# Applying a norm's factors behind the products instead of ahead of them, in a two-layer streaming encoder

## The chip, the cores and the metric

The kernel runs on one core of a Trainium2 chip. TensorE (PE) multiplies, VectorE (DVE), ScalarE (ACT) and GpSimd (POOL) work on tiles, and SyncE (SP) issues most of the loads. The metric is the time of one execution in microseconds; a run's time is a median over executions. Times of instructions are from one execution that the hardware profiler recorded.

## What is computed

Two groups of rows (512 prompt positions and 64 sample positions, 576 in all) go through two layers that share their weights. Cut to what matters here:

```python
def rmsnorm(x, g):
    y = xf * lax.rsqrt(jnp.mean(xf * xf, axis=-1, keepdims=True) + EPS)
    return (y * g)
...
h = x + 0.5 * rmsnorm(swiglu(rmsnorm(x, f1_pre), f1_up, f1_down), f1_post)      # FFN 1
mix, new = token_mix(rmsnorm(h, m_pre), ..., w_in, ...)                         # mixer
h = h + rmsnorm(mix, m_post)
h = h + 0.5 * rmsnorm(swiglu(rmsnorm(h, f2_pre), f2_up, f2_down), f2_post)      # FFN 2
e = pe @ ple_w
h = h + rmsnorm(e * sigmoid(rmsnorm(h, ple_pre) @ ple_gate_w), ple_post)        # PLE
```

The model width is 1024, the FFN width 2816. `swiglu` is silu(a) * b of two halves of one product. The mixer's input projection makes the inputs of four branches and four gates. All is float32 in and out.

## The kernel before

**Layout.** Activations lie with features on the partitions: `h` is 8 tiles (k = 0 to 7) of 128 features x 576 rows. A row's norm factor is therefore one number for each column, spread to all partitions by small matmuls.

**Products.** A weight unit is 1024 x 128 (8 tiles k). For the precision, weights and inputs are each split into a high and a low part (`whi`, `wlo`; `u_hi`, `u_lo`), and `products` (L598) runs high x high, high x low and low x high for each k, in two halves of 288 columns: 6 matmuls for each tile k, 48 for a unit. Units go through four slots: SP loads `wraw`, ACT rounds it to `whi` (`act_round`, L560), POOL subtracts to `wlo` (`split`, L2017; `wlo` lies where `wraw` was), PE multiplies, and its end (`unit_done`) frees the slot for the load of the unit four later. Products land in one of four pairs of PSUM banks.

**Norms.** At the end of FFN 1, mixer, FFN 2 and PLE stands a norm of that stage's result (`pe_norm_y`): ACT squares, DVE adds the squares, PE sums over partitions with a matrix of ones (`token_sums`, L630, 10 matmuls for a tile of 576 rows), ACT takes the root, DVE the reciprocal, PE spreads it (`spread`, L638, 10 matmuls). DVE then makes `uf` = y * gain * factor tile by tile (L846), and DVE or POOL add it to `h` (L838; POOL tiles 1, 3, 4, 6, DVE the rest). Right behind it stands the norm of the next stage's input (`pe_norm_h`): ACT squares each new tile of `h`, PE sums it (8 x 10 matmuls), root, reciprocal and spread again, DVE makes `uf` = h * gain * factor (L829, the factor read from PSUM), ACT copies it to `u_hi` (L747), and DVE (tiles 0, 3, 7) or POOL (1, 2, 4, 5, 6) subtracts to `u_lo` (L823). Only then do the first products of the stage have their tile; `wait_k` makes the first unit wait tile by tile. `keep_clock` issues dummy matmuls (L615) in pauses of PE.

**Stages.** The FFN's up loop runs 11 times over four units (a, b, a, b of two pairs): ACT takes silu of a's PSUM, DVE multiplies by b's PSUM, and splits into `s_hi`, `s_lo`; down units of 1024, 1024 and 768 rows follow. The mixer runs five projections (`FILL0`: two forget gates F, two queries Q, the first value V), each drained by ACT (`act_proj_some`, L928 and on), then the recurrent branch with further projections as fill. The order of every engine is written out by hand; an engine's instructions run in their order, with semaphore waits between engines.

**The start** of the first layer: SP loads the rows in five pieces and then the weights; PE transposes them (L456), DVE copies them to `h`, squares are added on DVE, and one `pe_norm_y` follows. 15 small loads of gains, taps and other rows are issued by ACT first of all.

Of the kernel before, what the change touches and what calls it, by code (L numbers as in the profile page):

```python
# [70 lines left out]
LO_POOL, LO_DVE = (1, 2, 4, 5, 6), (0, 3, 7)  # L71
ADD_POOL, ADD_DVE = (1, 3, 4, 6), (0, 2, 5, 7)
# [7 lines left out]

R_CONVB, R_LNG, R_LNB = range(3)
N_TAPS = DEPTH * CW * 2
N_ROWS = 9 * DEPTH
N_ROW_LOADS = 16
# [3 lines left out]
def trunk(nc, a, o):  # L88
    n_consts = [0]
    n_late = [0]  # L90
    with ExitStack() as ctx:
# [68 lines left out]


# [21 lines left out]
        hgs0 = rh("hgs0", [2, HD])  # L183
# [17 lines left out]
        rbc = Region(limit - 8192 - 32)  # L201
        sbk_c = rbc("sbk_c", [4, 256])
        sbv_c = rbc("sbv_c", [4, 256])
        assert rs.at <= limit - 8224
# [3 lines left out]
        spx = rb("spx", [2, 512])  # L208
        arg = rb("arg", [2, 512])

# [24 lines left out]
        rr = Region(ru.at)  # L235
        prow = rr("prow", [3, 128])
        prow_end = rr.at
        xtok = Region(prow_end)("xtok", [TB, D])
        otok = Region(ru.at + 3 * KD * T * 4)("otok", [TB, D])
        alibi_neg = Region(limit - 4096)("alibi_neg", [WINDOW + CHUNK])  # L240
# [10 lines left out]
        def halves(ap):  # L251
# [8 lines left out]
        turned = sem("turned")  # L260
        placed = sem("placed")
# [19 lines left out]
        h_ready_pool = sem("h_ready_pool")  # L281
        u_full = sem("u_full")
# [84 lines left out]
            h_ready: 16, h_ready_pool: 16, u_full: 32, u_high: 32, u_ready: 12, u_ready_pool: 20,  # L367
# [14 lines left out]
        ROW_BANKS = (0, 4, 5)  # L382

        def setup_sync(sp_):
            sp_.dma_start(xtok[0:DEC, NT, :], a["x_sample"][0]).then_inc(tok_loaded, 16)
            for c in range(4):
                f = slice(D // 4 * c, D // 4 * (c + 1))
                sp_.dma_start(xtok[:, 0:NT, f], a["x_prompt"][0].rearrange("(t p) d -> p t d", p=128)[:, :, f]).then_inc(x_loaded[c], 16)

# [56 lines left out]
        def setup_tensor(pe):  # L446
            pe.wait_ge(consts_done, 2)
            pe.wait_ge(tok_loaded, 16)
            for k in range(KD):
                if k % 2 == 0:  # L450
                    pe.wait_ge(x_loaded[k // 2], 16)
                if k >= 4:
                    pe.wait_ge(placed, k - 3)
                for t in range(TB):
                    n = min(128, T - 128 * t)
                    ins = pe.transpose(flat(k % 4)[:, 128 * t:128 * t + n], xtok[0:n, t, 128 * k:128 * k + 128], ident[0:n, 0:n])  # L456
                ins.then_inc(turned, 1)
# [6 lines left out]
        def setup_vector(dve, add_square):  # L464
            for k in range(KD):
                dve.wait_ge(turned, k + 1)
                dve.tensor_copy(h[:, k, :], flat(k % 4)).then_inc(placed, 1)
                if k:
                    add_square(k - 1)
# [1742 lines left out]
```

## Time and profile before

| | us |
|---|---|
| median of 3 runs | 3248.1 (3246.3 to 3248.9) |
| the profiled execution | 3254.2 |
| its span, first to last instruction | 3252.5 |

The page lists, for each engine, its busy time and share of the span. The chain of waits is the work that ended last, followed back from the last instruction; in order of time it reads as start, length, engine, operation and how many instructions were merged. The timeline lists instructions in order of time, merged where alike, with the idle time before them and what ended it. The table of stretches gives for each engine the busy time and number of instructions and then PEclk, the granted TensorE clock as a share of 2.4 GHz (0.50 is 1.2 GHz). TensorE's clock is recorded from 26.6 us on; before that the table shows 1.00 for want of a record. Matmuls overlap, so the time of a run of matmuls is read from start to start.

### The profile page before, as it was taken

The page shows a single profiled execution, that of the slowest core. Times are in us where ns is not written, and L with a number is a line of the kernel's source. Part 1 is how long each engine was busy: PE and PEld are TensorE (multiplying, and loading weights), DVE is VectorE, ACT ScalarE, POOL GpSimd, SP SyncE. Part 2 cuts the span into 40 slices and gives each one's busy share as a digit, 9 for nine tenths or more (in the row PEclk, how much of TensorE's full clock was granted, in tenths as well). Part 3 has the DMA queues.
Part 4 walks back from the last instruction along what each step waited for, and adds up shares of the span by engine and source line. Part 5 has one row for each costly group of instructions (what it writes and reads, how often), then busy time and mean ns, then how long its engine had stood idle before and what let it go on. Part 6 is the DMA issues. An engine that isn't in the chain of part 4 may idle for free.

```text
span 3252.5 us, 55941 instructions
## 1 busy us (share of the span) xinstructions
PE 3149.6 (97%) x24207; PEld 3034.4 (93%) x24207; DVE 964.3 (30%) x1417; ACT 1089.4 (33%) x1544; POOL 1179.3 (36%) x564
## 2 busy tenths in 40 slices
PE   8999999999999999999999999999998999999998
PEld 8999999996799999999999999999867999999997
DVE  3111024744344311101331110248434433111023
ACT  3223222335433323322433222323454333323233
POOL 5434333331133433433443333423212434333333
PEclk9999989999999999999999999999999999999999
DMA  3222212321122222232212222223111222222221
GB/s 102 80 82 82 83 55 63 87 69 48 40 72 79 59 84 83 78 90 80 65 53 83 84 81 80 62 62 92 56 48 46 78 79 59 84 81 87 83 69 62
DMA packets 455968, 236.46 MB, mean 73 GB/s; under 512 B 18630, under 2 KB 454150, under 8 KB 455814
## 3 DMA queue, kind: packets, MB, share of 16 engines
q1 hardware_dynamic: 445792, 227.05, 23.9%
q10 hardware_dynamic: 10022, 7.15, 0.7%
q8 instruction: 122, 2.00, 0.3%
q14 instruction: 32, 0.26, 0.0%
HBM read 228.53 MB, written 5.63 MB: 72 GB/s over the span
## 4 chain that ended last, share of the span: by engine, by line
PE 89%; DVE 5%; ACT 3%; POOL 1%; issue 1%; ACTq 1%; POOLq 0%; DVEq 0%
PE ps L598 79%; PE ps L630 3%; PE ps L1549 1%; PE ps L638 1%; DVE uf L829 1%; PE ps L1529 1%; PE ps L1567 1%; DVE u_lo L823 1%; PE ps L1868 1%; ACT u_hi L747 1%; POOL u_lo L823 1%; DVE kgate L1140 0%; PE ps L1553 0%; ACT ybr L1728 0%; PE ps L1391 0%
## 5 line engine op out<-in xcount | busy, mean ns | idle before, releaser
L2017 POOL TENSOR_TENSOR wlo<-wraw,whi 128x1024 fp32r<-128x1024 f32 (+1 forms) x432 | 1042.0, 2417 | 1918.2 <-ACT whi L560 1917.9
L598 PE MATMUL ps<-u_hi,whi 128*128 128x288 f32 x4800 | 1051.3, 300 | 43.7 <-POOL u_lo L823 11.8
L598 PE MATMUL ps<-u_hi,wlo 128*128 128x288 f32 x4800 | 1032.7, 296 | 0.0
L598 PE MATMUL ps<-u_lo,whi 128*128 128x288 f32 x4800 | 1032.6, 296 | 0.0
L598 PEld LDWEIGHTS ps<-u_hi,whi 128*128 128x128 f32 x4800 | 768.7, 189 | 80.9 <-issue 53.1
L598 PEld LDWEIGHTS ps<-u_lo,whi 128*128 128x128 f32 x4800 | 773.5, 189 | 0.0
L598 PEld LDWEIGHTS ps<-u_hi,wlo 128*128 128x128 f32 x4800 | 773.5, 189 | 0.0
L560 ACT ACTIVATE whi<-wraw 128x1024 fp32r<-128x1024 f32 (+1 forms) x432 | 449.5, 1040 | 562.9 <-PE ps L598 331.9
L872 DVE TENSOR_TENSOR sq<-sq,ps 128x576 f32<-128x576 f32 x88 | 66.4, 754 | 900.2 <-PE ps L598 900.2
L598 PE MATMUL ps<-s_hi,whi 128*128 128x288 f32 x1408 | 303.0, 296 | 0.0
L598 PE MATMUL ps<-s_lo,whi 128*128 128x288 f32 x1408 | 302.6, 296 | 0.0
L598 PE MATMUL ps<-s_hi,wlo 128*128 128x288 f32 x1408 | 302.6, 296 | 0.0
L598 PEld LDWEIGHTS ps<-s_hi,whi 128*128 128x128 f32 x1408 | 226.4, 189 | 0.3
L598 PEld LDWEIGHTS ps<-s_hi,wlo 128*128 128x128 f32 x1408 | 226.5, 189 | 0.0
L598 PEld LDWEIGHTS ps<-s_lo,whi 128*128 128x128 f32 x1408 | 226.3, 189 | 0.0
L560 ACT ACT_TABLE_LOAD x44 | 56.5, 1283 | 420.7 <-PE ps L598 420.7
L813 DVE TENSOR_TENSOR sqsum<-sqsum,sq 128x576 f32<-128x576 f32 x54 | 40.8, 756 | 473.7 <-ACT sq L726 473.7
L1321 DVE SCALAR_TENSOR_TENSOR yc<-zc,taps_all,yc 128x606 f32<-128x606 f32 x120 | 151.1, 1260 | 4.2
L726 ACT ACTIVATE sq<-ps 128x576 f32<-128x576 f32 x48 | 31.3, 652 | 283.6 <-PE ps L598 283.6
L630 PE MATMUL ps<-ones,sq 128*128 128x64 f32 x690 | 90.9, 294 | 6.2 <-ACT sq L726 5.9
L630 PEld LDWEIGHTS ps<-ones,sq 128*128 128x128 f32 x690 | 88.4, 209 | 8.2 <-ACT sq L726 6.8
L598 PE MATMUL ps<-m_split,whi 128*128 128x288 f32 x512 | 89.3, 296 | 0.3 <-DVE m_split L1765 0.3
(271 smaller groups left out, 2586.3 us busy)
## 6 DMA issues: line engine op xcount, KB each, us to landing
wraw<-in_ffn_up SPq DMA_DIRECT2D x176, 512.0 KB, 3.8
wraw<-in_w_in SPq DMA_DIRECT2D x104, 512.0 KB, 3.8
wraw<-in_ffn_down SPq DMA_DIRECT2D x64, 512.0 KB, 4.0
wraw<-in_ffn_down SPq DMA_DIRECT2D x32, 384.0 KB, 3.4
wraw<-in_w_out SPq DMA_DIRECT2D x16, 512.0 KB, 4.0
wraw<-in_ple_gate_w SPq DMA_DIRECT2D x16, 512.0 KB, 4.0
wraw<-in_w_branch SPq DMA_DIRECT2D x16, 256.0 KB, 2.7
xtok<-in_x_prompt SPq DMA_DIRECT2D x4, 512.0 KB, 6.2
```

Source lines behind the costliest of these rows:

```text
L560: act.activation(whi[:, i % SLOTS, 0:width(i)], wraw[:, i % SLOTS, 0:width(i)], ACT.Copy).then_inc(w_rounded, 1)
L598: ins = pe.matmul(ps[:, 2 * p + f, 0:HT], wt[:, part, w], x[:, k, HT * f:HT * f + HT], start=start and n == 0 and c == 0, stop=stop and n ...
L630: ins = pe.matmul(sum_at(p)[:, tb], x[:, t0:t0 + 128], ones[:, 0:SAME], start=start and tb == 0, stop=stop and tb == TB - 1, skip_group_ch ...
L638: ins = pe.matmul(flat(p)[:, t0:t0 + 128 - n0], col(tb), ident[:, n0:128], start=True, stop=True)
L747: act.activation(u_hi[:, k, :], uf[:, k, :], ACT.Copy).then_inc(u_high, 1)
L813: dve.tensor_tensor(sqsum[:], sqsum[:], sq[:, k % 2, :], ALU.add).then_inc(sq_added, 1)
L823: engine.tensor_tensor(u_lo[:, k, :], uf[:, k, :], u_hi[:, k, :], ALU.subtract).then_inc(signal, 1)
L829: dve.scalar_tensor_tensor(out=uf[:, k, :], in0=h[:, k, :], scalar=gains_all[:, n, L, k:k + 1], in1=flat(norm_pair(n)), op0=ALU.mult, op1= ...
L872: dve.tensor_tensor(halves(x), halves(x), pair(2 * q + 1), ALU.mult).then_inc(up_mul, 1)
L1321: ins = dve.scalar_tensor_tensor(out=yc[:, c, :], in0=zc[:, c, w:w + YW], scalar=wc, in1=yc[:, c, :], op0=ALU.mult, op1=ALU.add)
L1529: pe.matmul(ps[:, bk, 0:SEQ - 128 * kb], proj[hh, BK_ + c, 128 * kb:128 * kb + 128], proj[hh, BQ_ + c, 128 * kb:SEQ], start=True, stop=Tru ...
L2017: pool.tensor_tensor(wlo[:, i % SLOTS, 0:width(i)], wraw[:, i % SLOTS, 0:width(i)], whi[:, i % SLOTS, 0:width(i)], ALU.subtract).then_inc( ...
```

## The change

It leaves the arithmetic of a norm as it is but moves its factor, which is one number for each row and commutes with the product, behind the product, for FFN 1, FFN 2 and the mixer's first three projections.

- **Tiles.** `act_tiles` copies h * gain to `u_hi` as soon as a tile of `h` is there, then squares it; DVE's `tile_low` makes `u_lo` = h * gain - `u_hi`. PE's `pe_tiles` goes tile by tile: the sum of squares, then the tile's products of the first *two* units (into pairs 2 and 3); the spread of the factors stands ahead of the last tile. ACT copies the factors to SBUF as `rsb`.
- **FFN.** `gated` on DVE: a * rsb from PSUM, silu on ACT in place, * rsb, * b from PSUM, then the split. Units 0 to 3 stand outside the loops, which run 10 times. PE waits for `up_raw` ahead of the down units.
- **Mixer.** F, F+1 and the first Q run on raw tiles; DVE's `raw` multiplies them by `rsb` into `proj`. While Q runs, DVE makes the full `um` = h * gain * rsb and ACT overwrites `u_hi` behind PE (`u_spent`); `u_lo` is subtracted on DVE (0, 2, 4, 6, 7) and POOL (1, 3, 5). The second Q and all later units use it. ACT takes the sigmoids of F in `act_raw`, behind four cache loads. The recurrent state's load goes to `sqsum`'s place, and the load of `sbk_c` waits for `hg_norm` as well.
- **Residual.** POOL adds tiles 1 to 6, DVE 0 and 7, at all norms. PLE's own input norm stays as it was.
- **Weights around it.** The second unit's `act_round` and `split` stand ahead of the residual in place of behind it.
- **Start.** SP loads the first two units' weights between the rows' pieces; the first gain is loaded and transposed by itself, so `act_tiles` can begin; PE mixes transposes, sums (8 in place of 2) and the first unit's tiles. The other 15 row loads are issued by ACT behind the first rounds, and their transposes, copies and the bounds stand at the end of the first up loop.

```diff
-ADD_POOL, ADD_DVE = (1, 3, 4, 6), (0, 2, 5, 7)
+ADD_POOL, ADD_DVE = (1, 2, 3, 4, 5, 6), (0, 7)
+LO_POOL = {N_MPRE: (1, 3, 5), N_PPRE: (1, 2, 4, 5, 6)}
...
         def setup_sync(sp_):
...
+                if c < 2:
+                    src = a["ffn1_up"][bass.ds(0, 1), :, FF * c:FF * c + 128].rearrange("l (k p) n -> p (l k) n", p=128)
+                    sp_.wait_ge(unit_done, c + 1)
+                    sp_.dma_start(wraw[:, c, :].rearrange("p (k n) -> p k n", k=KD), src).then_inc(w_loaded[c], 16)
...
+                if n != N_F2POST:
+                    keep_clock(pe, 2, 2)
+                factors(pe, n)
...
+                keep_clock(pe, 8, 2)
+                pe.wait_ge(y_normed, 8 * (n // 2) + 1 + before(y_normed))
+                keep_clock(pe, 6, 2)
+                pe.wait_ge(t_high, tile_no(n + 1, 0, L) if n < N_PPOST else tile_no(N_F1PRE, 0, L + 1))
+                keep_clock(pe, 4, 2)
...
+            def pe_tiles(pe, n, i):
+
+                split_ready(pe, i + 1)
                 for k in range(KD):
+                    if k < KD - 1:
+                        h_sums(pe, n, k)
+                    if k == KD - 2:
+                        h_sums(pe, n, k + 1)
+                    if k == KD - 1:
+                        factors(pe, n)
+                    for j in range(2):
+                        tile_products(pe, n, i + j, 2 + j, k)
+
+            def pe_start(pe):
+
+                setup_tensor(pe, 0)
+                setup_tensor(pe, 1)
+                gain_tensor(pe)
+                setup_tensor(pe, 2)
+                h_sums(pe, N_F1PRE, 0)
+                setup_tensor(pe, 3)
+                h_sums(pe, N_F1PRE, 1)
+                split_ready(pe, 0)
+                for k in range(KD):
+                    tile_products(pe, N_F1PRE, 0, 2, k)
+                    if k < 4:
+                        setup_tensor(pe, 4 + k)
+                    if k < 6:
+                        h_sums(pe, N_F1PRE, 2 + k)
+                split_ready(pe, 1)
+                for k in range(KD):
+                    if k == 2:
+                        factors(pe, N_F1PRE)
+                    tile_products(pe, N_F1PRE, 1, 3, k)
...
+            def act_tiles(act, n, rounds):
 
                 for k in range(KD):
+                    wait_h(act, n, k)
+                    act.activation(u_hi[:, k, :], h[:, k, :], ACT.Copy, scale=gains_all[:, n, L, k:k + 1]).then_inc(t_high, 1)
+                    act_square(act, n, k, h[:, k, :])
+                    if k in rounds:
+                        act_round(act, rounds[k])
                 act_root(act, n)
+                act.wait_ge(factors_out, n + 1 + before(factors_out))
+                act.activation(rsb[:], flat(norm_pair(n)), ACT.Copy).then_inc(r_kept, 1)
...
+            def tile_low(dve, n, k, l):
+
+                dve.wait_ge(t_high, tile_no(n, k, l))
+                dve.scalar_tensor_tensor(out=u_lo[:, k, :], in0=h[:, k, :], scalar=gains_all[:, n, l, k:k + 1], in1=u_hi[:, k, :],
+                                         op0=ALU.mult, op1=ALU.subtract).then_inc(t_low, 1)
...
+            def dve_tiles(dve, n, src, n_in, l):
+
+                dve_rstd(dve, n)
+                for k in range(KD):
+                    norm_y_tile(dve, n, src, k)
+                    if k in ADD_DVE:
+                        add_to_h(dve, n, k, h_ready)
+                    if k >= 2:
+                        tile_low(dve, n_in, k - 2, l)
+                tile_low(dve, n_in, KD - 2, l)
+                tile_low(dve, n_in, KD - 1, l)
...
+                    dve.tensor_tensor(halves(x), pair(up_pair(2 * q)), halves(rsb[:]), ALU.mult).then_inc(up_raw, 1)
+                    dve.wait_ge(silu_done, it * 2 + (at + 1) + before(silu_done))
+                    dve.tensor_tensor(x, x, rsb[:], ALU.mult).then_inc(silu_scaled, 1)
+                    dve.wait_ge(silu_scaled, it * 2 + (at + 1) + before(silu_scaled))
+                    dve.wait_ge(unit_done, it * 4 + done(u0 + 2 * q + 1))
+                    dve.tensor_tensor(halves(x), halves(x), pair(up_pair(2 * q + 1)), ALU.mult).then_inc(up_mul, 1)
...
+            RAW_AT = (2, 3, 0)
+
+            def pe_mixer_in(pe):
+                pe_tiles(pe, N_MPRE, U0_PROJ)
+                i = U0_PROJ + 2
+                split_ready(pe, i)
+                for k in range(KD):
+                    ins = products(pe, i % SLOTS, u_hi, u_lo, (k,), k, RAW_AT[2], k == 0, k == KD - 1)
+                    ins.then_inc(u_spent if k < KD - 1 else unit_done, 1)
+                i = U0_PROJ + 3
+                split_ready(pe, i)
+                pe.wait_ge(r_kept, N_MPRE // 2 + 1 + before(r_kept))
+                products(pe, i % SLOTS, u_hi, u_lo, range(KD), 0, 1, True, True, wait_k=u_tile_ready(pe, N_MPRE)).then_inc(unit_done, 1)
+                pe.wait_ge(proj_raw, 3 + before(proj_raw))
+                for t in range(4, FILL0):
+                    pe_proj(pe, t)
+
+            def act_mixer_in(act):
+                act_tiles(act, N_MPRE, {2: U0_PROJ + 2})
+                act_round(act, U0_PROJ + 3)
+                for k in range(KD):
+                    u_high_tile(act, N_MPRE, k)
+                act_round(act, U0_PROJ + 4)
+
+            def act_raw(act):
+                for t in (F_, F_ + 1):
+                    act.wait_ge(proj_raw, t + 1 + before(proj_raw))
+                    act.activation(kgate[:, t, :], proj[:, t, :], ACT.Sigmoid, scale=-1.0)
+                    act.activation(proj[:, t, :], proj[:, t, :], ACT.Sigmoid).then_inc(proj_out, 1)
+                act.wait_ge(proj_raw, 3 + before(proj_raw))
+                act.activation(proj[:, Q_, 0:16], proj[:, Q_, 0:16], ACT.Copy).then_inc(proj_out, 1)
+                next_proj[0] = 3
+
+            def dve_mixer_in(dve):
+                dve_factors(dve, N_MPRE)
+
+                def full(k):
+                    dve.scalar_tensor_tensor(out=um[:, k, :], in0=h[:, k, :], scalar=gains_all[:, N_MPRE, L, k:k + 1], in1=rsb[:],
+                                             op0=ALU.mult, op1=ALU.mult).then_inc(u_full, 1)
+
+                def raw(t):
+                    dve.wait_ge(unit_done, done(U0_PROJ + t))
+                    dve.tensor_tensor(halves(proj[:, t, :]), pair(RAW_AT[t]), halves(rsb[:]), ALU.mult).then_inc(proj_raw, 1)
+
+                full(0)
+                full(1)
+                low(dve, N_MPRE, 0, u_ready)
+                full(2)
+                full(3)
+                low(dve, N_MPRE, 2, u_ready)
+                full(4)
+                full(5)
+                low(dve, N_MPRE, 4, u_ready)
+                full(6)
+                full(7)
+                raw(0)
+                raw(1)
+                low(dve, N_MPRE, 6, u_ready)
+                low(dve, N_MPRE, 7, u_ready)
+                raw(2)
...
                 act.wait_ge(outs, 32 + before(outs))
+                act.wait_ge(hg_norm, 2 + before(hg_norm))
...
                 straight(U_UP, U0_PROJ)
-                split(U0_PROJ)
+                straight(U0_PROJ, U0_PROJ + 2)
                 pool_residual(pool, N_F1POST)
-                split(U0_PROJ + 1)
+                straight(U0_PROJ + 2, U0_PROJ + 4)
                 pool_apply(pool, N_MPRE)
-                straight(U0_PROJ + 2, U0_FFN2 + 1)
+                straight(U0_PROJ + 4, U0_FFN2 + 2)
                 pool_residual(pool, N_MPOST)
```

## Rows read from the trace of the kernel before

**Rows 1.** The page, engine shares: busy us, share of the span, instructions.

```profile
PE 3149.6 (97%) x24207; PEld 3034.4 (93%) x24207; DVE 964.3 (30%) x1417; ACT 1089.4 (33%) x1544; POOL 1179.3 (36%) x564
```

**Rows 2.** The chain of waits, entry of FFN 2, first layer: start, us, engine, what.

```profile
1092.12 1.54 DVE uf L846 x2
1095.10 9.46 PE ps L630 x80
...
1116.85 400.25 PE ps L598 x3000
```

**Rows 3.** The chain of waits, the mixer's two entries.

```profile
458.90 1.54 DVE uf L846 x2
461.88 16.14 PE ps L630 x80
...
499.94 19.45 PE ps L598 x144
...
2074.74 1.54 DVE uf L846 x2
...
2108.13 19.46 PE ps L598 x144
```

**Rows 4.** The chain of waits, the first long run of products.

```profile
36.94 417.84 PE ps L598 x3132
```

**Rows 5.** Timeline, PE at the entry of FFN 2: start, us, line, operation, tiles, count.

```profile
1090.75 1.33 PE L638 MATMUL ps<-ident,rcol 128*128 128x128 f32 x10
1091.92 2.00 PE L615 MATMUL ps<-ident,ones 128*128 128x128 f32 x16
```

**Rows 6.** The chain of waits, products and sums in turn in the PLE stage.

```profile
1551.59 1.64 PE ps L1868 x12
1553.23 4.41 PE ps L630 x40
```

**Rows 7.** Timeline, DVE, ACT and POOL at the entry of FFN 2.

```profile
1108.15 0.76 DVE L823 TENSOR_TENSOR u_lo<-uf,u_hi 128x576 fp32r<-128x576 f32 x1
...
1109.66 0.69 ACT L747 ACTIVATE u_hi<-uf 128x576 fp32r<-128x576 f32 x1 [0.82 <-DVE uf L829]
...
1115.37 1.42 POOL L823 TENSOR_TENSOR u_lo<-uf,u_hi 128x576 fp32r<-128x576 f32 x1
...
1115.40 2.01 DVE L823 TENSOR_TENSOR u_lo<-uf,u_hi 128x576 fp32r<-128x576 f32 x1 [0.75 <-ACT u_hi L747]
```

**Rows 8.** Timeline, ACT and POOL at the second layer's mixer entry.

```profile
2100.06 0.40 ACTq L1793 DMA_DIRECT2D hgs<-in_state_hgrn  x1
...
2101.45 0.69 ACTq L1796 DMA_DIRECT2D swv_c<-in_cache_swa_v  x1
2102.17 1.28 ACT L928 ACT_TABLE_LOAD   x1 [4.19 <-issue]
...
2105.69 2.38 POOL L2017 TENSOR_TENSOR wlo<-wraw,whi 128x1024 fp32r<-128x1024 f32 x1 [6.27 <-ACT whi L560]
```

**Rows 9.** Timeline, PE at the start.

```profile
5.68 10.76 PE L456 MATMUL ps<-ident,xtok 128*128 128x128 f32 x40 [5.68 <-DMA xtok<-in_x_prompt]
...
21.19 2.34 PE L630 MATMUL ps<-ones,sq 128*128 128x64 f32 x10
...
26.43 2.55 PE L615 MATMUL ps<-ident,ones 128*128 128x128 f32 x20
```

**Rows 10.** PE at the lower clock: timeline of products; stretch: busy (x), PEclk, DMA share, GB/s.

```profile
883.71 0.68 PE L598 MATMUL ps<-o_lo,whi 128*128 128x288 f32 x2
884.19 0.68 PE L598 MATMUL ps<-o_hi,wlo 128*128 128x288 f32 x2
...
470.00:474.00 4.00, 4.00 (x21) 0.50 0.00 0
```

**Rows 11.** Timeline, DVE and POOL at the last residual.

```profile
3233.16 1.54 DVE L846 SCALAR_TENSOR_TENSOR uf<-e,gains_all,ps 128x576 f32<-128x576 f32 x2 [1.42 <-PE ps L638]
...
3236.90 5.11 POOL L838 TENSOR_TENSOR h<-h,uf 128x576 f32<-128x576 f32 x3 [0.26 <-DVE uf L846]
```

## What I predict, and how

> **What bounds the kernel now.** I read the page's engine shares first: the tensor engine (PE) is busy for 97% of the span [rows 1]. So only two things can move the time: stretches in which PE does no products, and stretches in which its products run slowly. The chain of waits shows where the first are. In the loops it is products all the way (3000 products in 400.25 us, 0.1334 each, so 6.4 for a unit of 48 [rows 2]), and it leaves PE, or falls back to small matmuls, at every norm. The entry of FFN 2 in the first layer [rows 2] stands for three. Call t0 the start of the first residual operation, 1092.12. Then come the residual, 80 matmuls of square sums (9.46, 0.118 each), the second norm, and the input split tile by tile; tile 6 of the first unit starts at 1116.85. From there 60 products are left in the first two units: 8.0 us, so they end 32.7 after t0. The same pair of lines, 24.7 apart, stands at two more entries (layer 2, FFN 1 and FFN 2). The two mixer entries [rows 3] end their first five units 60.5 and 52.9 after their t0 (499.94 + 19.45 - 458.90, and 2108.13 + 19.46 - 2074.74). The 7.6 between them is the clock: 80 sums took 16.14 in the first. At the kernel's start tile 6 begins at 36.94 [rows 4], so two units end at 44.9.
>
> **FFN entries (three).** Up to t0 nothing changes. After it PE gets a chain of its own. The spread of the factors starts at 1090.75 and 16 dummy matmuls follow from 1091.92 in 2.00 us [rows 5]; now there are 36 (18 calls), at 0.125 each 4.5 us, to t0+4.3. Then eight times a sum (1.18) and a tile's 12 products. A stretch of the PLE stage has just this alternation, 12 products in 1.64 and sums right behind them [rows 6], so I take 1.62. With one spread (1.2): 4.3 + 8 x 2.8 + 1.2 = 27.9. What feeds it is faster. POOL's adds take 1.42, a DVE subtract 0.76, an ACT copy 0.69 [rows 7]; POOL and DVE block one another (the subtract issued 0.03 after a POOL one took 2.01, its own 0.76 behind the other's end), so a tile costs add plus subtract, 2.2 at most, under PE's 2.8. The first tile is ready at about t0+4.4, hidden by the dummies. **Gain 32.7 - 27.9 = 4.8 each, 14.4 in all**; 6 each if a dummy costs 0.11, 4 if each handover costs 0.1.
>
> **Mixer entries (two).** T, the end of the first two units, is again t0+27.9. Unit 2 still runs on raw tiles, to T+6.4. Unit 3 needs the fully normalized input, and here the work has grown: 8 normalizing operations on DVE that now read two SBUF tensors (h and rsb; before, the factor came from PSUM), 5 DVE subtracts, and on POOL a weight split (2.4 [rows 8]) and 3 subtracts. Taken as excluding one another [rows 7], 13 x 0.7 + 2.4 + 3 x 1.4 = 15.7 in one row, from T-0.9, and two PSUM products of 0.75 stand in DVE's queue ahead of the last two subtracts: the last tile is ready at T+16.3, and unit 3 ends at T+17.1, not T+12.8. Unit 4 waits for the third proj_out, and that is behind ACT's queue: last high tile T+14.3, a weight round 1.05, the four cache DMA issues 2.1, the sigmoid table 1.3 [rows 8], four sigmoids and a copy 2.4: T+21.3. PE is idle for four of those microseconds; the first mixer entry lost the clock behind a pause shorter than the 3.0 between its t0 and its first sum [rows 3], so I take a fall here too. Back-to-back products then start 0.24 apart [rows 10], and I add 2.2 to unit 4's 6.4. End: 27.9 + 21.3 + 8.6 = 57.8. **First layer -2.7, second +4.9.** Bounds: without exclusion DVE ends by T+10.4 and ACT's chain gives T+14 with no fall of the clock, 48.3 in all; above, 3 more for a longer fall.
>
> **The start.** Eight square sums come to PE in place of two, and they are mixed with transposes and products. As it was [rows 9]: first transposes at 5.68 behind the input's DMA, 10.76 for eight tiles (1.34 each); a sum of 10 matmuls takes 2.34, some 2.15 without the last one's tail; only at 26.43 do dummies run at 0.128 each. New order: four transposes and two sums, held once by ACT's first square at about 10.3 (the gain row is turned behind two tiles, then copied, then a high tile and the square of 0.7 each), end at 16.0. Then unit 0: 8 x 1.45 (six products at 0.24) + 4 x 1.34 + 6 x 2.15 = 29.9 if the clock stays low, to 45.9. Sums alone left it low: 470 to 474 is busy for 4.00 of 4.00 us at 0.50 [rows 10], and so did transposes and sums from 5.68 to 23.5; the dense spread and dummies behind them lifted it. This loop is transposes and sums for most of its time, work beside which the level stayed low, so I stay with that level until the products run unbroken, from 43 on; at a rise at 47.5, unit 1 has 1.1 tiles behind it, then 6.9 x 0.8 + 1.1: 54.1. **Cost 9.2** against 44.9. With a rise at 20 the same counts at 0.8, 1.18 and 1.34 end at 43.5, a gain of 1.4. The weights ahead of x tiles cost nothing in this: the second x chunk comes one 512 KB load later, and PE is behind with its own work from then on.
>
> The Trainium skill, TensorE: Matmul & The Clock Gate, Part 1, says that sustained matmul activity releases the clock. By that rule the start would run at 2.4 GHz soon after its first transposes, and the sum would be about 11 lower; the busy 4 us at 0.50 [rows 10] speak against it, since there the engine was never idle.
>
> **The end.** POOL gets six of eight residual adds in place of four. After the last norm nothing covers them: t0 is 3233.16, POOL's last add ended at 3242.01 [rows 11]. Six at 1.4 from t0+2.2, with one DVE add between them: t0+11.3, **2.4 later** (1.8 to 3.2), and 22 transposes and the output still follow. At the two PLE entries the same delay hides behind PE's e products and sums; uncovered it would be 2.4 each.
>
> **What I cost at nothing.** (1) FFN gate: DVE has two operations more per pair of units, five at 0.76 plus blocks of 2.4 or less; a pair is 12.8 of PE. ACT's silu waits for the first of them, 0.8 behind the unit, while ACT rounds a weight (1.05) anyway. (2) PE's new wait for up_raw ahead of the down units: the last raw product belongs to the last but one unit, 6.4 earlier. (3) The 15 row loads move on ACT from before the first square to behind the first rounds, at 0.52 an issue [rows 8] 7.8 us; queued behind them are the first silu and the round of unit 4. The first gate then ends some 9 to 10 after unit 1; unit 4 asks for it at 12.8. If that margin goes, it costs its excess once. (4) Bounds and row transposes move to the end of the first up loop: 0.9 of PE, which it also paid before; ACT's Exp and table loads there sit ahead of a round that PE needs two units later. (5) The second unit's split moves ahead of the residual on POOL, its round ahead of the last copy on ACT: both have the last down or output units as cover. (6) ACT's wait for hg_norm ahead of the sbk_c load: the projection copies ahead of it in that queue end later than the factors do.
>
> **Sum.** -14.4 - 2.7 + 4.9 + 9.2 + 2.4 = -0.6 against the profiled execution's 3254.2 (span 3252.5 and 1.7 around it): 3253.6. That execution is 6.1 above the median of the runs, so I carry the difference over: 3247.5, say 3247. If the runs don't have the first mixer's slow sums, its gain turns to +4.9 and this is 3255.
>
> **Rivals.** (a) The clock rises early in the start, since products are a new kind of work there: 10.6 less, 3237. For it: unbroken products raise the clock. Against it: nothing in the stretch is unbroken. (b) The mixer entry is not held by DVE and POOL's exclusion: 9.5 less each, 3228; half of it, 3237. Against: the 2.01 [rows 7]. (c) Slower: a tile loop is entered with the clock low, and its sums keep it there, as they did at the first mixer entry. Place: the gap between the last dummies and the first sum, where the first mixer entry lost it [rows 3]. Price, at the lower level throughout: 8 x (2.15 + 2.9) + 2.2 + 4.3 = 46.9 in place of 27.9, 19 for one such entry: 3266. It decides if the gap grows past what the dummies fill; 18 of them speak against it, one fall in five entries before speaks for it. (d) The loops don't overlap as written, because a tile's inputs are late: 2.2 against 2.8 excludes it on these rows.
>
> **How the numbers follow.** Forecast 0.43, (a) 0.23, (b) 0.12, (c) 0.22. About 0.2%, 6.5 us, is what a measurement of this kernel tells from no change. (a) and (b) are faster by more: 0.35. (c) is slower: 0.22. The range, 3230 to 3262, takes in (a), the half of (b), the upper costs at start, mixer and end together (+8), and leaves out part of (b) and of (c). The forecast's own range is 3240 to 3256.
>
> **What would show it.** FFN entries: two units end at t0+27 to 29, and PE has no gap in the loop. Mixer: unit 4 starts 18 to 22 behind the first two units, with DVE operations of 1.4 to 2 beside POOL's. Start: sums of unit 0 at 0.21 per matmul, granted clock at 1.2 GHz until 46 to 50; two units done at 52 to 56. End: POOL's last add about 11 after its t0. The forecast is wrong if the start's products run at 0.134 before 30, or if any of the five later loops shows 0.24.

## The result: 20 us faster, where no change was forecast

The changed kernel takes 3228.6 us (median of 5 runs, 3225.1 to 3234.2) against 3248.9 beside it: ratio 0.992, 95% interval 0.990 to 0.994. Two later comparisons, both on one chip, gave 0.991 (0.990 to 0.993) and 0.990 (0.988 to 0.993), which are 29 and 32 us: the kernel before had medians of 3257.7 and 3260.2 there. The profiled execution has 3228.6, its span 3226.8; that of before had 3254.2 and 3252.5.

The page, shares of the engines. DVE has 283 us more to do (964.3 before [rows 1]), ACT 95 us less, and PE, the bound, 12 us less:

```profile
PE 3137.4 (97%) x24248; PEld 3030.4 (94%) x24248; DVE 1246.9 (39%) x1584; ACT 993.9 (31%) x1482; POOL 1213.0 (38%) x556
```

The timeline of DVE gives the new t0 of the entries (start, us, line, operation); they answer to 458.90, 1092.12, 2074.74 and 3233.16 [rows 2, 3, 11]:

```profile
456.07 0.81 DVE L972 SCALAR_TENSOR_TENSOR uf<-y,gains_all,ps 128x576 f32<-128x576 f32 x1 [1.42 <-PE ps L683]
...
1084.86 0.81 DVE L972 SCALAR_TENSOR_TENSOR uf<-y,gains_all,ps 128x576 f32<-128x576 f32 x1 [1.42 <-PE ps L683]
...
2053.71 0.81 DVE L972 SCALAR_TENSOR_TENSOR uf<-y,gains_all,ps 128x576 f32<-128x576 f32 x1 [1.42 <-PE ps L683]
...
3205.46 0.81 DVE L972 SCALAR_TENSOR_TENSOR uf<-e,gains_all,ps 128x576 f32<-128x576 f32 x1 [1.42 <-PE ps L683]
```

Cut at these points, the span divides as follows:

| stretch | before | after | change | forecast |
|---|---|---|---|---|
| start and FFN 1, to the first mixer's t0 | 458.90 | 456.07 | -2.8 | +9.2 |
| mixer entry, layer 1, t0 to the end of unit 4 | 60.49 | 53.57 | -6.9 | -2.7 |
| rest of that mixer | 572.73 | 575.22 | +2.5 | 0 |
| FFN 2 and PLE, layer 1, to PLE's norm | 528.76 | 522.60 | -6.2 | -4.8 |
| that norm, to layer 2's t0 | 7.17 | 5.43 | -1.7 | 0 |
| FFN 1, layer 2 | 446.69 | 440.82 | -5.9 | -4.8 |
| mixer entry, layer 2 | 52.85 | 53.46 | +0.6 | +4.9 |
| rest of that mixer | 572.47 | 571.32 | -1.2 | 0 |
| FFN 2 and PLE, layer 2 | 533.10 | 526.97 | -6.1 | -4.8 |
| last t0 to the end | 19.34 | 21.34 | +2.0 | +2.4 |
| sum | | | -25.7 | -0.6 |

The chain of waits shows the entries (start, us, engine, count). At FFN 2, 36 dummies take 4.07 (0.113 each), then a tile takes 2.71 (1095.34 to 1098.05), with no pause of PE in between; from the last tile on, 12 products finish the two units, at 1110.02 + 12 x 0.1333 = 1111.62, t0+26.8 (before: t0+32.7 [rows 2]). At the mixer, DVE's `um` and `u_lo` are the chain up to the fifth unit:

```profile
36.93 273.65 PE ps L643 x2052
...
500.69 8.95 PE ps L643 x54
...
1084.82 4.07 PE ps L660 x36
1095.34 1.65 PE ps L643 x12
1098.05 1.65 PE ps L643 x12
...
1110.02 393.65 PE ps L643 x2952
...
2090.83 2.62 DVE um L1123 x2
2094.78 3.51 DVE u_lo L951 x2
2098.33 8.84 PE ps L643 x54
...
3207.08 4.58 POOL h L994 x3
3213.02 3.24 POOL h L994 x2
3216.30 4.93 PE ps L2327 x22
```

The timeline of PE at the start. A sum of ten matmuls takes 2.39 until 16.5 and 1.33 from 22 on; in between it went from 1.2 to 2.4 GHz. The record of the granted clock begins with the rise, at 19.34, 3.1 us behind the start of the first products:

```profile
14.12 2.39 PE L675 MATMUL ps<-ones,sq 128*128 128x64 f32 x10
16.28 0.83 PE L643 MATMUL ps<-u_hi,whi 128*128 128x288 f32 x2
...
19.14 1.41 PE L675 MATMUL ps<-ones,sq 128*128 128x64 f32 x10
...
20.72 0.42 PE L643 MATMUL ps<-u_lo,whi 128*128 128x288 f32 x2
...
21.98 1.33 PE L675 MATMUL ps<-ones,sq 128*128 128x64 f32 x10
```

### The profile page after: what moved, and what is told of

It reads as the page before. It is cut to its first block, busy times and chain, and to the rows that moved or that the text cites. A ratio compares the mean times of both kernels' runs of the same rounds, so it can differ in the third digit from the quotient of the medians.

```text
span 3226.8 us, 55975 instructions
## 1 busy us (share of the span) xinstructions
PE 3137.4 (97%) x24248; PEld 3030.4 (94%) x24248; DVE 1246.9 (39%) x1584; ACT 993.9 (31%) x1482; POOL 1213.0 (38%) x556
## 4 chain that ended last, share of the span: by engine, by line
PE 91%; DVE 4%; ACT 2%; POOL 1%; issue 1%; ACTq 0%; DMA 0%; SPq 0%; POOLq 0%; DVEq 0%
PE ps L643 81%; PE ps L675 3%; PE ps L1781 1%; PE ps L683 1%; PE ps L1761 1%; PE ps L1799 1%; PE ps L660 1%; PE ps L2098 1%; DVE u_lo L951 1%; DVE kgate L1372 0%; DVE um L1123 0%; PE ps L1785 0%; ACT ybr L1960 0%; PE ps L1623 0%; PE ps L1770 0%
## 5 line engine op out<-in xcount | busy, mean ns | idle before, releaser
L2250 POOL TENSOR_TENSOR wlo<-wraw,whi 128x1024 fp32r<-128x1024 f32 (+1 forms) x432 | 1082.6, 2515 | 1892.8 <-ACT whi L600 1892.4
L1034 DVE TENSOR_TENSOR sq<-sq,rsb 128x576 f32<-128x576 f32 x88 | 211.0, 2397 | 96.0 <-ACT sq L895 96.0
L1032 DVE TENSOR_TENSOR sq<-ps,rsb 128x576 f32<-128x576 f32 x88 | 66.8, 759 | 346.4 <-PE ps L643 341.9
L994 POOL TENSOR_TENSOR h<-h,uf 128x576 f32<-128x576 f32 x48 | 82.3, 1747 | 79.3 <-DVE uf L972 79.3
```

Source lines behind the costliest of these rows:

```text
L994: engine.tensor_tensor(h[:, k, :], h[:, k, :], uf[:, k, :], ALU.add).then_inc(signal, 1)
L1032: dve.tensor_tensor(halves(x), pair(up_pair(2 * q)), halves(rsb[:]), ALU.mult).then_inc(up_raw, 1)
L1034: dve.tensor_tensor(x, x, rsb[:], ALU.mult).then_inc(silu_scaled, 1)
L2250: pool.tensor_tensor(wlo[:, i % SLOTS, 0:width(i)], wraw[:, i % SLOTS, 0:width(i)], whi[:, i % SLOTS, 0:width(i)], ALU.subtract).then_inc( ...
```

## The experiments

All edits are to the changed kernel, unless the text says otherwise. Its own repeats gave 3228.6 and 3227.8.

> The changed kernel, a second profile and more times beside the three mixer runs. The first profile ended the five units of a mixer entry 53.6 and 53.5 us behind t0 (t0: start of the first residual operation), with the clock at 1.2 GHz for 6.83 us in both, and the start's clock rose at 19.34; in another kernel with the same start it rose at 24.07. Expected: the mixer entries within 1 us of 53.5 again; the start's two units at 41 to 45.

Measured: five units end at t0+53.6 (500.97 + 9.05 - 456.38) and t0+53.3 (2095.73 + 8.71 - 2051.10), and the start's clock rises at 19.87. In the 12 profiles with this start the rise lay at 18.5 to 19.9 in eight and at 24.1 to 24.8 in four; the later one, some 8 us behind the first products, costs 2 to 3 us.

**What the clock did in the kernel before.** Two runs of the kernel before: once unedited, once with

```diff
-                    keep_clock(pe, 8, 2)
+                    keep_clock(pe, 14, 2)
```

> The kernel before, a second profile. The first one had its square sums at the lower clock behind the first layer's mixer entry (80 sums in 16.14 us in place of 9.46) and a fall to 1.2 GHz at the start of layer 2 (1620.66 to 1627.49). Theory 1: these falls hang on what the tensor engine did before and come back at the same places; then the changed kernel's gain at the first mixer entry (6.9 us from t0 to the end of the fifth unit) is a gain in every execution. Theory 2: they fall where they like; then the 80 sums take 9.46 here, the entry ends its five units 52.9 behind t0 in place of 60.5, and that part of the gain belongs to one execution alone.

> The kernel before with 14 dummy calls in place of 8 behind the spread of a residual's factors, so that the 1.18 us in which the tensor engine waits for the first square sum are filled; nothing else of the change. If that pause loses the clock at the first mixer entry (80 sums in 16.14 and 16.40 us, 9.45 at the other entries), the sums take 9.45 there too and the kernel is 6 to 7 us faster than before (ratio 0.998), so that about a quarter of the change's gain is the clock alone. If the sums themselves lose it, whatever stands ahead of them: 16 us again, and no change or 0.2 us more for each entry.

The unedited kernel lost the clock at the same places again (80 sums in 16.40 at the first mixer entry, and a fall at 1620.49 ahead of layer 2). With the dummies, the chain of waits of the edited kernel has:

```profile
458.64 3.18 PE ps L615 x28
461.82 9.29 PE ps L630 x80
...
492.11 19.44 PE ps L598 x144
...
1647.79 407.43 PE ps L598 x3132
```

Five units end 52.9 behind t0 (458.68), not 60.5, and the kernel is 7.4 us faster by the medians: ratio 0.9977 (0.9959 to 0.9995). So the 6.9 at the first mixer entry are the clock's, and filling a pause of 1.18 us would have had them without the change. (The profiled execution gained more, 12.6 in its span; the last row alone is 10.4 of it, see the end.)

**What raised it at the start.** First, all transposes and sums ahead of the products:

```diff
-                setup_tensor(pe, 2)
-                h_sums(pe, N_F1PRE, 0)
-                setup_tensor(pe, 3)
-                h_sums(pe, N_F1PRE, 1)
+                for k in range(2, KD):
+                    setup_tensor(pe, k)
+                    h_sums(pe, N_F1PRE, k - 2)
+                h_sums(pe, N_F1PRE, KD - 2)
+                h_sums(pe, N_F1PRE, KD - 1)
                 split_ready(pe, 0)
                 for k in range(KD):
                     tile_products(pe, N_F1PRE, 0, 2, k)
-                    if k < 4:
-                        setup_tensor(pe, 4 + k)
-                    if k < 6:
-                        h_sums(pe, N_F1PRE, 2 + k)
```

> The changed kernel, but at the start the tensor engine does all transposes and square sums first and the first unit's products behind them. In the changed kernel the clock rose at 19.34 us, about 3 us behind the first products (16.28), and two units ended at 41.55. Theory A, products mixed in lift the clock: without them transposes (8 x 1.34) and sums (8 x 2.15) stay slow to about 34, the clock rises some 3 us into the products, and two units end at 48 to 51, so the kernel takes 7 to 9 us more than the changed one (about 3236 to 3238). Rival B, transposes and sums without a pause lift it as well, products or not: the rise comes near 19 again, and two units end at 41 to 43, no change in the time. Rival C, it takes what it took in the kernel before, where the clock rose at 26.64: two units end at about 45, 3 to 4 us more.

The chain of waits of that kernel:

```profile
10.57 2.32 PE ps L675 x10
...
27.94 6.59 PE ps L675 x30
34.53 9.07 PE ps L643 x60
44.66 273.65 PE ps L643 x2052
```

Sums at 0.22 to 0.23 a matmul up to 34.5, the clock up at 36.69, and the long run 7.7 later than in the changed kernel (44.66 against 36.93): theory A. 24 us of transposes and sums without a pause stayed at 1.2 GHz; the same work with a unit's products in it did not, in any of the 12 profiles. The median is 3237.5, ratio 0.993.

Then dummies (`ones` by `ident`) from 1.87 us on, ahead of the input: 16 calls (each is two matmuls in the trace); 8 calls, with 4 more ahead of the first product; 10, with 4 more behind the gain's transpose and 6 ahead of the first product. The last two also round the first units one tile earlier:

```diff
+                pe.wait_ge(consts_done, 3)
+                for _ in range(16):
+                    pe.matmul(ps[:, 2, 0:128], ones[:], ident[:], start=True, stop=True)
...
-                    act_tiles(act, n, {1: 0, 3: 1})
+                    act_tiles(act, n, {0: 0, 2: 1})
```

> The changed kernel with 16 dummy matmuls on the tensor engine ahead of the first transposes, from about 2.0 us, while it waits for the input (5.71). If any unbroken work of the tensor engine lifts the clock, it is up at 5 to 6 us: transposes of 0.80 and sums of 1.18 from there, and two units end at 36 to 38 in place of 41.55, the kernel 4 to 5 us faster than the changed one (3224). If only products lift it, or the wait for the second piece of the input (0.66 at 9.31) drops it again, the rise stays near 19 and nothing changes (3228 to 3229).

> The changed kernel's start with 8 dummy calls (16 matmuls) in place of the 16 calls of the run before, so that they end before the input is there (5.7 us), 4 calls more ahead of the first product, and the first two units' rounds one tile earlier on ACT. In the run with 16 calls the clock rose at 6.67 but fell at 16.91, behind a pause of 1.47 us in which the tensor engine waited for the first unit's low part (POOL), and stayed at 1.2 GHz to 23.73. Theory: it is the pause that lost it. Then here the clock is up from 6 or 7 us to the end of the start, and the 24 merged products that begin at 32.62 to 32.93 in the changed kernel begin at 28 to 30: 3 to 4 us less, 3224 to 3226. Rival: dummies lift the clock only for a while and the start's own mix, with its waits for the input's pieces, can't hold it: a fall between 10 and 20 again, and no gain or up to 1.5 us lost.

> The start of the run with 8 dummy calls, whose clock rose at 5.90 and fell at 9.31 behind two waits for the input of 0.95 and 1.01 us. Here 10 calls stand ahead of the input, 4 behind the gain's transpose and 6 ahead of the first product, so that the tensor engine has work in all three places. If the pauses are what drops the clock, it stays up from 6 us on and the 24 merged products begin at 28 to 30 in place of 32.5 to 33.2: 3 to 4 us less than the changed kernel. If it falls again between 9 and 20 with the pauses filled, pauses are not the cause, and the start gains nothing (33 to 35).

The dummies lifted the clock at 6.67, 5.90 and 4.87. It fell at 16.91, 9.31 and 11.70, each time in or up to 2 us behind a pause of about 1 us or more, and came back at 23.73, 19.55 and 18.52. The timelines of PE, 16 calls first:

```profile
15.93 0.53 PE L643 MATMUL ps<-u_hi,whi 128*128 128x288 f32 x2 [1.47 <-POOL wlo L2250]
...
18.02 2.39 PE L675 MATMUL ps<-ones,sq 128*128 128x64 f32 x10
```

8 calls:

```profile
6.60 1.62 PE L485 MATMUL ps<-ident,xtok 128*128 128x128 f32 x10 [0.95 <-DMA xtok<-in_x_prompt]
...
9.39 1.41 PE L485 MATMUL ps<-ident,xtok 128*128 128x128 f32 x5 [1.01 <-DMA xtok<-in_x_prompt]
```

10 calls:

```profile
9.69 0.86 PE L485 MATMUL ps<-ident,xtok 128*128 128x128 f32 x5 [1.05 <-DMA xtok<-in_x_prompt]
...
12.89 2.39 PE L675 MATMUL ps<-ones,sq 128*128 128x64 f32 x10
```

The faster PE only waits longer, for the input or for POOL's split, and the clock falls there. The run that the changed kernel begins at 36.93 began at 38.30, 38.05 and 37.34: nothing gained. The medians are 3231.5, 3227.0 and 3225.5, with ratios of 0.991, 0.991 and 0.990 to the kernel before, as for the changed kernel. That pauses are the cause isn't proved, since each of the three kernels kept one.

**What held it at the entries.** The 18 dummy calls behind the spread taken out, with the two waits that stand between them:

```diff
-                keep_clock(pe, 8, 2)
...
-                keep_clock(pe, 6, 2)
...
-                keep_clock(pe, 4, 2)
```

> The changed kernel without the 36 dummy matmuls behind each spread of a residual's factors, so the tensor engine stands idle for some 4 us ahead of each of the five tile loops. My third rival of the prediction says that a tile loop entered at the lower clock stays there: 19 us for each of five, about 95 more than the changed kernel (3323). Against it stands the start of the changed kernel, where the same mix of sums and products went from 1.2 to 2.4 GHz by itself some 3 us behind the first products: then a loop begins slow and costs 2 to 4 each, 10 to 20 in all (3239 to 3249). If 4 us of pause don't drop the clock, nothing changes (3228).

The median is 3247.7, ratio 0.9967 (0.995 to 0.998): 19 us of the gain gone by the medians; in the profile 17.0, of which the start's rise at 24.07 has 2.4 and the last norm 2.7. The chain of waits at the first mixer entry: one sum and one tile at the lower level, then 1.65 a tile.

```profile
461.55 2.36 PE ps L675 x10
463.92 2.99 PE ps L643 x12
...
471.16 1.65 PE ps L643 x12
```

From the norm's sums to the loop's last sums the five entries took 2.2, 2.3, 4.0, 0.9 and 2.4 more. The loop lifts its own clock, as the start did. The prediction's rival (c) was right that a loop can be entered with the clock low, and wrong that its sums keep it there and in its price, 19 for one entry.

**One unit in the loop instead of two.**

```diff
-                    for j in range(2):
-                        tile_products(pe, n, i + j, 2 + j, k)
+                    tile_products(pe, n, i, 2, k)
+                for k in range(KD):
+                    tile_products(pe, n, i + 1, 3, k)
```

> The changed kernel with one unit in the tile loops (sum and 6 products for each tile, 1.85 us) and the second unit behind the loop. Theory: the loop of the changed kernel is bound by the tensor engine (2.71 a tile, no pause), and its feed by DVE and POOL runs at about 1.9 a tile; with one unit the loop follows the feed, its last tile is there at about t0+18.2 and the spread has less work in front of it, so two units end at t0+27 to 28.5 in place of 26.6: 0.5 to 2 for each of five entries, 3 to 9 us in all (3231 to 3237). Rival 1: the feed is faster than the loop needs: no change. Rival 2: the loop's small waits drop the clock: 3 or more for each entry, over 15 in all.

The median is 3253.5, ratio 0.9996 (0.998 to 1.001): the gain is gone. At FFN 2 a tile takes 1.91 (1096.51 to 1098.42 in the timeline). That is what a sum and six products need and also the pace of the feed, whose DVE subtracts start 1.9 apart. At tile 5 the feed falls behind and PE waits, while DVE takes 4.36 for its last three subtracts:

```profile
1096.51 1.22 PE L675 MATMUL ps<-ones,sq 128*128 128x64 f32 x10
...
1098.42 1.22 PE L675 MATMUL ps<-ones,sq 128*128 128x64 f32 x10
...
1107.57 0.53 PE L643 MATMUL ps<-u_hi,whi 128*128 128x288 f32 x2 [2.20 <-DVE u_lo L967]
```

DVE's timeline there:

```profile
1104.61 4.36 DVE L967 SCALAR_TENSOR_TENSOR u_lo<-h,gains_all,u_hi 128x576 fp32r<-128x576 f32 x3
```

Two units end at t0+29.2 at the FFN entries (1112.71 + 54 x 0.1333 - 1090.74), 2.4 later than with two; at the mixer entries the clock falls behind that wait (475.22 and 2079.48) and they lose 5.7 and 5.9 (at the FFN entries the same wait did not drop it). The 2.4 goes the way of the theory, beyond its 0.5 to 2; the mixer's part is rival 2. The second unit is what hides the feed.

**The mixer entry, cut into its chains.** The subtracts first; the loads behind the sigmoids; both; then the subtracts first and no wait for ACT:

```diff
+                low(dve, N_MPRE, 6, u_ready)
+                low(dve, N_MPRE, 7, u_ready)
                 raw(0)
                 raw(1)
-                low(dve, N_MPRE, 6, u_ready)
-                low(dve, N_MPRE, 7, u_ready)
...
+                act_raw(act)
                 act.dma_start(hgs0, a["state_hgrn"][bass.ds(L, 1), 0].rearrange("l (c a) k v -> (a k) (l c) v", a=2)).then_inc(cache_in, 16)
...
-                act_raw(act)
...
-                if t >= 2:
+                if t > 4:
                     pe.wait_ge(proj_out, t - 1 + before(proj_out))
```

> The changed kernel with DVE's two subtracts for the last two tiles of the mixer's input (L951, 3.5 us for both beside POOL's weight split) ahead of its two products of raw results (1.4), not behind them. Theory A, the fifth unit is held by two chains that end within 0.5 us of one another (in the changed kernel unit 3 ended at 2099.94, while ACT's last copy for the fifth unit ended at 2099.41): unit 3 ends some 3 us earlier, but the fifth unit then waits for ACT's chain, and the entry gains 0.5, or up to 2 if the shorter pause keeps the clock up. Theory B, DVE's and POOL's exclusion alone sets the entry: 3 to 4 us less per entry (five units end at t0+50), 6 to 8 in all. Theory C, that of the prediction, ACT's queue alone sets it: 0.

> The changed kernel with the four cache loads on ACT's queue (2.1 us to issue) behind the sigmoids of F, not ahead of them. Theory A, two chains of nearly the same length: 0 to 0.5 less for each entry, as unit 3 still ends at T+19.6 (T: end of the first two units). Theory B, DVE and POOL alone: 0. Theory C, ACT's queue alone, as the prediction had it: 2.1 less for each entry, five units end at t0+51.4.

> Both edits. Theory A: 2.5 to 4.5 less for each entry, more than the two edits by themselves give together (five units end at t0+49 to 51), 5 to 9 in all. Theory B: the same as the subtracts' move alone. Theory C: the same as the loads' move alone, 2.1 each.

> The changed kernel with the two last subtracts ahead of the raw products, as in the run where the fifth unit then waited 3.49 us for ACT's last sigmoid and copy; and the fifth unit no longer waits for ACT, only for DVE's third raw product, which frees its PSUM banks. If the two chains (DVE with POOL, and ACT with its table and sigmoids) are all that held the entry, the fifth unit starts at about t0+43.5 in place of t0+46.4, the clock stays up, and the first small matmuls of the recurrent branch start at t0+50 to 51 in place of 54.2: 3 to 4 for each entry, 6 to 8 in all, 3221 to 3223. If the branch behind it then waits for ACT's sigmoids or DVE's gates, part of it is given back there: 2 to 4 in all.

From t0 to the first products behind the fifth unit, both layers:

| kernel | layer 1 | layer 2 | median |
|---|---|---|---|
| changed | 54.3 | 54.2 | 3228.6 |
| subtracts first | 53.2 | 54.7 | 3231.2 |
| loads later | 54.4 | 54.1 | 3228.8 |
| both | 52.7 | 55.2 | 3225.7 |
| subtracts first, no wait for ACT | 51.3 | 51.4 | 3219.3 |

The first four rows were run side by side, the last on another chip. Other profiles with an unedited mixer have 54.1 to 55.5 (the second repeat 55.5 and 54.7, where 54.2 was expected), so a microsecond in the middle rows says little. The last row came back at 51.2 to 51.4 in all three later profiles with its edit.

With the subtracts first, PE's timeline in layer 2 has ACT in DVE's place, as theory A says, and the clock falls in that pause:

```profile
2097.38 0.67 PE L643 MATMUL ps<-u_hi,whi 128*128 128x288 f32 x2 [3.49 <-ACT proj L1116]
```

Both edits together did not give the 2.5 to 4.5 of theory A: PE still waits 3.01 for ACT (2094.86), since the loads cost ACT only 0.5, not 2.1; they are issued while ACT rounds a weight. Only without the wait does the entry shorten in both layers, by 3.0 and 2.8, and the clock stays up. What ends last then is POOL's weight split (chain of waits of that kernel):

```profile
497.43 2.38 POOL wlo L2250
499.94 6.62 PE ps L643 x48
507.29 1.78 PE ps L643 x12
```

**The end, and all together.** The last residual shared as before:

```diff
+END_POOL, END_DVE = (1, 3, 4, 6), (0, 2, 5, 7)
...
-                for k in ADD_POOL:
+                for k in (END_POOL if n == N_PPOST and L == DEPTH - 1 else ADD_POOL):
                     add_to_h(pool, n, k, h_ready_pool)
```

> The changed kernel with the last norm's residual shared as in the kernel before (POOL tiles 1, 3, 4, 6, DVE the other four). My price for POOL's two more adds was 2.4 us (1.8 to 3.2); the spans from t0 to the end gave 2.0 (21.3 against 19.3). Expected: t0 to the end of the span 19.3 again, 2 us less. Rival: the tail is held by the tensor engine's clock (1.2 GHz for 13.65 us in the changed kernel there, 6.83 in the kernel before), not by the adds: less than 1 us.

From t0 (3203.94) to the end of the span 19.3, as forecast: 2.1 less, the adds. The median is 3224.9.

> The three edits together: start, mixer entries, end. If they add up: 3 to 4, 6 to 8 and 2 less than the changed kernel, 3215 to 3218, a ratio to the kernel before of 0.987 or so. If one cost that is taken away at one place comes back behind it (a later wait, a fall of the clock): 3220 to 3225.

> The changed kernel with the two edits that gained: DVE's last subtracts ahead of the raw products and the fifth unit free of ACT's chain (both mixer entries: 2.9 each measured), and the last residual shared as before (2.1 measured). If they add up: 3217 to 3220, ratio to the kernel before 0.988 to 0.989. If not, 3221 to 3225.

> The changed kernel, beside the next one on the same chip: 3226 to 3231, the start's clock up near 19 or near 24.5, the mixer entries at t0+54.2, t0 of the last residual to the end 21.3.

> The changed kernel with both mixer entries and the last residual edited, once more. If the stretches add up as the profiles show them (2 x 2.9 and 2.1): 7 to 9 us less than the changed kernel on this chip. If the time is given back elsewhere: under 4.

With the start's edit: 3221.3 (0.9899). Without it: 3223.2 (0.9897), with the start's rise at 24.84, and, beside the changed kernel on one chip, 3222.1 (3217.9 to 3224.9) against 3227.8 (3224.3 to 3230.7); their profiled spans 3216.2 and 3225.1. It beats both kernels; by the medians it gains 5.6 of the 7.9 that its stretches show, which is between the two expectations. The two sums before it missed theirs: neither 3215 to 3218 nor 3217 to 3220 came, and the mixer edits alone had 3219.3. Differences of 2 us between these kernels are within the scatter of their executions.

## Why the prediction was wrong

**The start** is the step that failed most, 12.0 of the 25.1 us between -0.6 and -25.7. The order of work came as described, but I stayed "with that level until the products run unbroken". The row that I rested this on, sums alone at 0.50 [rows 10], was right, and the kernel with all sums first bears it out for 24 us. What didn't follow is that sums with a unit's products between them behave like sums. The sign that the prediction named for being wrong came: products ran at 0.13 from 20.4 on. With the rise at 19.34 the two units ended at 41.7 (36.93 + 36 x 0.1333), earlier still than rival (a)'s 43.5. The forecast had (a) at 0.23; it should have been the likeliest. That the total, 3228.6, is just what rival (b) asked for is chance: the two mixer entries missed their terms by 8.5 of the 25.1, not by 19.

**FFN entries**: mechanism right, size off. Loop bound by PE, first tile under the dummies, no gap: t0+26.8 in place of 27.9, because a dummy took 0.113 (I took 0.125) and a tile 2.71 (2.8). The stretches gained 6.2, 5.9 and 6.1 in place of 4.8. DVE and POOL did hold one another: beside POOL's adds DVE's subtracts start 1.9 apart, which is the feed's pace for a tile, under PE's 2.71.

**Mixer entries**: 53.5 in place of 57.8. The loop gave 1.3 of it. The ACT chain that I had at T+21.3 ended at T+19.1 (2099.41 - 2080.3): its loads cost 0.5 in place of 2.1, they ran beside the round. The DVE row was later than I had it, T+18.0 in place of T+16.3: it counted one weight split of POOL's, and there were two, the second, for the fifth unit, beside the last two subtracts. Without a split beside them, as in the kernel with both edits, these two took 1.59 in place of 3.58. Timelines of DVE, POOL and ACT, layer 2:

```profile
2094.70 3.58 DVE L951 TENSOR_TENSOR u_lo<-um,u_hi 128x576 fp32r<-128x576 f32 x2
...
2080.61 2.88 POOL L2250 TENSOR_TENSOR wlo<-wraw,whi 128x1024 fp32r<-128x1024 f32 x1 [10.73 <-ACT whi L600]
...
2095.19 2.48 POOL L2250 TENSOR_TENSOR wlo<-wraw,whi 128x1024 fp32r<-128x1024 f32 x1 [2.36 <-ACT whi L600]
...
2094.07 1.04 ACT L600 ACTIVATE whi<-wraw 128x1024 fp32r<-128x1024 f32 x1
...
2095.61 1.28 ACT L1113 ACT_TABLE_LOAD   x1 [0.50 <-issue]
...
2099.21 0.20 ACT L1116 ACTIVATE proj<-proj 128x16 f32<-128x16 f32 x1
```

So rival (b) was wrong about the exclusion, and unit 3 and ACT's chain met within half a microsecond, unit 3 last (2099.94). I had ACT's queue as what holds the fifth unit; here it was DVE and POOL's row, and ACT's close behind. The fall of the clock that I charged came, 2094.65 to 2101.47, at 1.6 in place of 2.2: the 54 products from 2098.33 on took 8.84, where 54 x 0.1333 are 7.2. In the table of stretches:

```profile
2080.30:2094.65 14.35, 12.23 (x86) 11.29 (x85) 13.39 (x13) 6.21 (x10) 8.67 (x4) 1.00 0.39 112
2094.65:2101.47 6.82, 4.95 (x19) 4.60 (x20) 6.79 (x9) 5.54 (x9) 2.48 (x1) 0.50 0.14 38
```

In layer 1 the gain is the 7.6 of slow sums [rows 3] less the same 0.6 that layer 2 loses. I had doubted whether the runs had those sums; they came back in a second profile of the kernel before.

**PLE's norm ahead of layer 2**, where I had no term, gave 1.7, and that is the clock again: its 20 sums took 4.50 before, 4.50 again in the second profile, and 2.42 in the changed kernel. Why the fall comes later there was not tested. The chains of waits, before and after:

```profile
1620.88 4.50 PE ps L630 x20
...
1607.46 2.42 PE ps L675 x20
```

**The end** cost 2.0 (2.4 forecast), and giving the adds back returned 2.1. **What I cost at nothing** stayed at nothing: the stretch from PLE's first sums to its norm is 84.56 in both kernels, and the first gate's multiply stood at 47.08 with unit 4 not waiting. The rests of the two mixers moved by +2.5 and -1.2. Of the +2.5, 1.4 are the slower pace of 432 products (last section). In other profiles of this kernel, and of the one that only has the mixer edited, that stretch took 570 to 573, with the falls of the clock at other places.

**From the profile to the median.** I subtracted 6.1, as the profiled execution stood that far above the three runs. In the later comparisons the kernel before had medians of 3254 to 3261: the three runs were low, not the profile high. Without that step the forecast would have been 3253.6, so the 3247 lies nearer to the measured time for a reason that did not hold.

## What to carry to other kernels

Where the clock decides, ask which work lifts it: here products did and dummies did, and rows of small sums never did, so a stretch's level with products mixed in can't be read from a stretch without them. A second unit of work beside the chain that feeds it hides the chain's pace and its small waits; with one unit the whole gain was gone. And before a chain is charged for a queued DMA issue, see whether the engine computes beside it.

## What the runs showed of the hardware that was not expected

Unbroken products run at two paces at a granted clock of 1.00 throughout. The 3132 products of FFN 1 took 417.84 in the kernel before [rows 4], in both layers, and in layer 2 of the one with more dummies 407.43: 0.1334 and 0.1301 each, 10.4 us in one stretch. In the changed kernel the same 432 products of the mixer took 57.61 in layer 1 and 56.17 in layer 2. What sets the pace stayed open.

At the end the clock fell in every kernel, and its transposes ran at either level (22 in 3.61 to 4.96), which moved the span by less than the adds did.
